# x1 through memory, and three more experts' weights in its room, in a one-core mixer and MoE layer

## The reference, cut to what matters

```
h  = rmsnorm(x, g_mix);  z = h @ w_in                 # 8 groups of 256 columns
mix = concat(conv A, pooling B, conv C, spatial gating D)
x1 = x + mix @ w_out                                  # the projection
h2 = rmsnorm(x1, g_ffn)
group = argmax(h2 @ rg_w);  two experts of its eight by h2 @ re_w
moe = sum over the two experts of gate * (silu(h2 @ w_gate[e]) * (h2 @ w_up[e])) @ w_down[e]
y  = rmsnorm(x1 + moe, g_final)
```

## Time and profile before

| | |
|---|---|
| median of 3 runs | 653.86 us (653.0 to 654.6) |
| profiled execution | 653.97 us, its span 652.1 us |
| busy: TensorE, VectorE, ScalarE, GpSimd | 557.4, 489.3, 278.6, 106.7 us |
| DMA | 116.33 MB, mean 178 GB/s |
| mean granted TensorE clock | 0.940 of full |

### The profile page before, as it was taken

One profiled execution on the slowest core, in us unless ns is written; L12 is line 12 of the kernel. 1 busy time (PEld: TensorE's weight loads), 2 busy tenths in 40 slices (PEclk: granted clock), 3 DMA queues, 4 the chain that ended last, 5 costly groups with the idle time before them and its releaser, 6 DMA issues.

```text
span 652.1 us, 10367 instructions
## 1 busy us (share of the span) xinstructions
PE 557.4 (85%) x3411; PEld 488.3 (75%) x3411; DVE 489.3 (75%) x758; ACT 278.6 (43%) x425; POOL 106.7 (16%) x150
## 2 busy tenths in 40 slices
PE   3899999999999998999999835999999999995000
PEld 2899999998898896888888525888888888883000
DVE  4947997999998668366655766888888888883597
ACT  5742112320313354312112125777777777773132
POOL 4300002000000000000000002233344444441000
PEclk9999999999999999999999956999999999999555
DMA  8660210111203103454211288799999999931884
GB/s 321 145 133 16 65 33 23 44 54 34 64 9 131 64 7 131 187 213 151 90 64 49 79 292 259 241 330 374 324 351 365 394 382 377 349 140 28 333 334 155
DMA packets 51445, 116.33 MB, mean 178 GB/s; under 512 B 8435, under 2 KB 26744, under 8 KB 50296
## 3 DMA queue, kind: packets, MB, share of 16 engines
q1 hardware_dynamic: 42899, 92.82, 41.1%
q0 software_dynamic: 6656, 17.84, 8.0%
q10 hardware_dynamic: 1828, 4.96, 2.1%
HBM read 99.75 MB, written 20.68 MB: 185 GB/s over the span
## 4 chain that ended last, share of the span: by engine, by line
PE 57%; DVE 19%; ACT 2%; DMA 2%; issue 2%; POOL 0%; POOLq 0%; DVEq 0%; ACTq 0%
PE ps L1942 14%; PE ps L2060 9%; PE ps L1765 8%; PE ps L2039 5%; PE ps L2020 5%; PE ps L2038 5%; PE ps L2040 5%; DVE at_x L1693 4%; PE ps L1983 2%; DVE at_mixP L1236 2%; DVE at_x L1701 2%; DVE at_hT L1196 1%; PE ps L1721 1%; DVE at_lnsq L1421 1%; DMA at_opair_p<-scratch_out 1%
## 5 line engine op out<-in xcount | busy, mean ns | idle before, releaser
L1765 PE MATMUL ps<-at_hT,at_ring 128*128 128x384 f32 x936 | 165.7, 333 | 1.1 <-ACT at_wk L641 1.1
L1765 PEld LDWEIGHTS ps<-at_hT,at_ring 128*128 128x128 f32 x936 | 155.8, 188 | 6.5 <-issue 5.0
L1942 PE MATMUL ps<-at_hT,at_mring 128*128 128x512 f32 (+1 forms) x432 | 102.6, 393 | 1.9 <-DVE at_mring L1389 1.2
L1942 PEld LDWEIGHTS ps<-at_hT,at_mring 128*128 128x128 f32 (+1 forms) x432 | 77.3, 182 | 21.1 <-DVE at_mring L1389 1.6
L2038 PE MATMUL ps<-at_whi,at_hTm 128*128 128x256 f32 x280 | 81.8, 292 | 0.0
L1236 DVE SCALAR_TENSOR_TENSOR at_mixP<-at_uc,sb_par,at_mixP 128x1024 f32<-128x1024 f32 x60 | 77.4, 1289 | 2.1
L2040 PE MATMUL ps<-at_whi,at_hTm_lo 128*128 128x256 f32 x280 | 78.8, 281 | 0.0
L1583 DVE TENSOR_TENSOR at_hTm_lo<-ps,at_hTm 128x1024 fp32r<-128x1024 f32 x35 | 42.9, 1225 | 21.6 <-ACT at_hTm L881 21.6
L1590 DVE TENSOR_TENSOR at_wlater_lo<-at_wlater,at_whi 128x1024 fp32r<-128x1024 f32 x40 | 49.0, 1226 | 9.6 <-ACT at_whi L889 7.9
L2020 PEld LDWEIGHTS ps<-sb_ident,at_xg 128*128 128x128 f32 x280 | 37.3, 190 | 24.6 <-issue 21.6
L2038 PEld LDWEIGHTS ps<-at_whi,at_hTm 128*128 128x128 f32 x280 | 53.5, 191 | 0.2 <-issue 0.2
(11 more groups left out here) (247 smaller groups left out, 859.4 us busy)
## 6 DMA issues: line engine op xcount, KB each, us to landing
at_wlater<-in_expert_w_gate SPq DMA_DIRECT2D x20, 512.0 KB
at_wlater<-in_expert_w_up SPq DMA_DIRECT2D x20, 512.0 KB
at_wlater<-in_expert_w_down SPq DMA_DIRECT2D x20, 512.0 KB
at_raw<-in_w_in SPq DMA_DIRECT2D x16, 512.0 KB, 3.9
at_opair_p<-scratch_out SPq DMA_DIRECT2D x8, 1024.0 KB, 12.4
at_wfirst<-in_expert_w_gate SPq DMA_DIRECT2D x15, 512.0 KB
at_wfirst<-in_expert_w_up SPq DMA_DIRECT2D x15, 512.0 KB
at_wfirst<-in_expert_w_down SPq DMA_DIRECT2D x15, 512.0 KB
```

Of the source, the lines that this page charges most:

```text
L1765: mm = pe.matmul(ps[:, bank + r, 0:t1 - t0], w[:, wpart, k * P:(k + 1) * P], hT[:, hpart, k, t0:t1], start=(m, wpart, hpart) == (0, 0, 0), ...
L1942: mm = pe.matmul(ps[0:n, b + r, :], mring[:, 1 - i % 2, mpart, k * P:k * P + n], wo[:, wpart, k, r * 512:(r + 1) * 512], start=(c, mpart, ...
```

## The change

x1 of each tile is written to a new tensor in memory (`xs`) right behind the tile's h. Once a tile's store has landed, its room, which is exactly one matrix wide, takes one matrix of experts 0 to 2 (`first_matrix`; tile t takes matrix t mod 3 of expert t div 3). The ring of eight slots starts with expert 3: expert b lies in slot (b-3) mod 8. Experts 3 to 5 are loaded at the first three tiles, 6 when the projection is done, 7 behind the last tile, 8 to 10 when the first gather has landed, and the rest as before when the expert eight earlier is done. When the last weights are issued and expert 2 is done, SyncE reads the nine tiles of x1 back to where they were, and VectorE waits for each of them in the last stage.

```
+            def store_rows(i):
                 sp.wait_ge(s["h2_ready"], i + 1)
                 sp.dma_start(hs[i * P:i * P + rows(i), :], wk[0:rows(i), i % 2, 0:D])...
+                sp.dma_start(xs[i * P:i * P + rows(i), :], x1[0:rows(i), i, :])\
+                    .then_inc(x1_stored[i % 2], 16)
+
+            def first_matrix(t):
+                sp.wait_ge(x1_stored[t % 2], 16 * (t // 2 + 1))
+                load_matrix(0, t // 3, t // 3, t % 3)
...
             for i in range(TILES):
                 if i == LAST:
                     sp.wait_ge(s["o_done"], TILES)
-                    expert_block(0, FIRST, FIRST, first=True)
-                store_h2(i)
+                    load_expert(0, 2 * FIRST, 2 * FIRST)
+                store_rows(i)
                 if i < FIRST:
-                    expert_block(0, i, i, first=True)
+                    load_expert(0, FIRST + i, FIRST + i)
+                if i >= 1:
+                    first_matrix(i - 1)
                 if i + 2 < TILES:
                     reload_x(i + 2)
...
-            for j in range(FIRST + 1, FIRST + 3):
-                expert_block(0, j, j, first=True)
+            load_expert(0, 2 * FIRST + 1, 2 * FIRST + 1)
+            first_matrix(LAST)
 
             sp.wait_ge(gath[0], 16)
-            for j in range(FIRST + 3, LAP):
-                expert_block(0, j, j, first=True)
-            with sp.Fori(1, NE // LAP) as i:
+            for j in range(2 * FIRST + 2, FIRST + LAP):
+                load_expert(0, j, j)
+            for j in range(FIRST, LAP):
+                expert_block(1, j, LAP + j)
+            with sp.Fori(2, NE // LAP) as i:
                 for j in range(LAP):
                     expert_block(i, j, i * LAP + j)
...
+            sp.wait_ge(s["d_done"], FIRST)
+            for n in range(2):
+                sp.wait_ge(x1_stored[n], 16 * ((TILES + 1 - n) // 2))
+            for i in range(TILES):
+                sp.dma_start(x1[0:rows(i), i, :], xs[i * P:i * P + rows(i), :]).then_inc(x_in[i], 16)
             sp.wait_ge(s["moe_done"], 1)
...
                     dve.wait_ge(pair_in[i], 16)
+                    dve.wait_ge(x_in[i], 48)
```

Which room and which semaphore belong to a block follows from new functions (`wexp(i, j)`, `weights_in(i, j)`), used by all engines:

```
+        def once(i, j):
+            return isinstance(i, int) and i * LAP + j < FIRST
+        def weights_in(i, j):
+            if once(i, j):
+                return once_in[j], 16, 0
+            return w_in_sem[(j - FIRST) % LAP], 16, i + (j - FIRST) // LAP
```

More of the change, by code:

```diff
@@ L145, in build_layer, with slot_of, wexp, wexp_lo @@
         o_xg = o_ring
[L146 to L155, removed]
+        wring = [at("wring_x", [P, FIRST, 3 * D], o_x1), at("wring_h", [P, LAP - FIRST, 3 * D], o_hT),
+                 at("wonce", [P, FIRST, 3 * D], o_mix)]
+        wring_lo = [at("wring_x_lo", [P, FIRST, 3 * D], o_x1, F32R),
+                    at("wring_h_lo", [P, LAP - FIRST, 3 * D], o_hT, F32R),
+                    at("wonce_lo", [P, FIRST, 3 * D], o_mix, F32R)]
+        def once(i, j):
+            return isinstance(i, int) and i * LAP + j < FIRST
+        def slot_of(parts, i, j):
+            if once(i, j):
+                return parts[2][:, j, :]
+            n = (j - FIRST) % LAP
+            return parts[0][:, n, :] if n < FIRST else parts[1][:, n - FIRST, :]
+        def wexp(i, j):
+            return slot_of(wring, i, j)
+        def wexp_lo(i, j):
+            return slot_of(wring_lo, i, j)
         whi = [at("whi0", [P, 2, KC // 2, FF], o_raw + D * 2, F32R),
@@ L161, in half @@
             return x[:, 0:2 * D].rearrange("p (g k f) -> p g k f", g=2, k=KC)[:, :, h * 4:h * 4 + 4, :]
-        def wexp_lo(j):
-            j %= LAP
-            return wfirst_lo[:, j, :] if j < FIRST else wlater_lo[:, j - FIRST, :]
         xg = at("xg", [P, XG, D], o_xg)
@@ L286, in build_layer @@
         hs = nc.dram_tensor("scratch_h", [NT, D], F32, kind="Internal").ap()
+        xs = nc.dram_tensor("scratch_x1", [NT, D], F32, kind="Internal").ap()
         orow = nc.dram_tensor("scratch_out", [2 * NT, D], F32, kind="Internal").ap()
@@ L308, in build_layer @@
         w_in_sem = [sem(f"expert_in{i}") for i in range(LAP)]
+        once_in = [sem(f"first_experts_in{i}") for i in range(FIRST)]
+        x1_stored = [sem(f"x1_stored{i}") for i in range(2)]
         gath = [sem(f"gathered{i}") for i in range(XG)]
@@ L413, in zf_wait, with weights_wait @@
             eng.wait_ge(s["zf_" + Z_USER[n]], nth(Z_USER, n))
-        def lap(i, j):
-            return i + j // LAP
+        def weights_in(i, j):
+            if once(i, j):
+                return once_in[j], 16, 0
+            return w_in_sem[(j - FIRST) % LAP], 16, i + (j - FIRST) // LAP
+        def weights_wait(eng, i, j):
+            arrived, each, turn = weights_in(i, j)
+            eng.wait_ge(arrived, 3 * each * turn + 3 * each)
         def result_out(eng, i):
@@ L513, in _, with load_matrix, load_expert, expert_block @@
                 load_piece(NPIECE + c)
[L515 to L526, removed]
+            def load_matrix(i, j, e, m):
+                w = ("expert_w_gate", "expert_w_up", "expert_w_down")[m]
+                src = a[w][0, bass.ds(e, 1), :, :].rearrange("o (q k) f -> q (o k f)", q=P)
+                sp.dma_start(wexp(i, j)[:, m * D:(m + 1) * D], src).then_inc(weights_in(i, j)[0], 16)
+            def load_expert(i, j, e):
+                for m in range(3):
+                    load_matrix(i, j, e, m)
+            def expert_block(i, j, e):
+                sp.wait_ge(s["d_done"], i * LAP + j - LAP + 1)
+                load_expert(i, j, e)
             def reload_x(i):
@@ L532, in reload_x @@
                 load_x(i, x1)
-            def store_h2(i):
+            def store_rows(i):
                 sp.wait_ge(s["h2_ready"], i + 1)
@@ L885, in expert_whi @@
                 b = i * LAP + j
-                act.wait_ge(w_in_sem[j % LAP], 48 * lap(i, j) + 48)
+                weights_wait(act, i, j)
                 if not (isinstance(b, int) and b < 1):
                     act.wait_ge(s["gu_done" if h else "gu_half"], b)
-                nc.scalar.activation(whi[h][:], half(wexp(j), h), ACT.Copy).then_inc(s[f"w_hi{h}"], 1)
+                nc.scalar.activation(whi[h][:], half(wexp(i, j), h), ACT.Copy).then_inc(s[f"w_hi{h}"], 1)
             def expert_silu(i, j):
@@ L1589, in expert_wlo @@
                 dve.wait_ge(s[f"w_hi{h}"], b + 1)
-                v.tensor_tensor(half(wexp_lo(j), h), half(wexp(j), h), whi[h][:].bitcast(F32),
+                v.tensor_tensor(half(wexp_lo(i, j), h), half(wexp(i, j), h), whi[h][:].bitcast(F32),
                                 ALU.subtract).then_inc(s[f"w_lo{h}"], 1)
@@ L2035, in expert_GU @@
                         pe.wait_ge(s[f"w_lo{h}"], b + 1)
-                    high, low = whi[h][:, :, k % 4, :], half(wexp_lo(j), h)[:, :, k % 4, :]
+                    high, low = whi[h][:, :, k % 4, :], half(wexp_lo(i, j), h)[:, :, k % 4, :]
                     x, x_low = hTm[:, j % 2, k, :], hTm_lo[j % 2][:, k, :]
@@ L2059, in expert_D @@
                     q = 2 * D + r * 512
-                    mm = pe.matmul(ps[:, 5 + r, :], actT[:, j % 2, :], wexp(j)[:, q:q + 512],
+                    mm = pe.matmul(ps[:, 5 + r, :], actT[:, j % 2, :], wexp(i, j)[:, q:q + 512],
                                    start=True, stop=True)
```

## The result

The changed kernel takes 656.65 us (median of 6 runs, 655.79 to 657.21) against 653.43 for the one before (6 runs, 652.91 to 654.6). The ratio is 1.0047, 95% interval 1.0037 to 1.0057: it is 3.1 us slower. The forecast of no change, the likeliest case, did not happen; the case beside it did, at the place that it named.

A forecast was written before the change was run, and what follows sets the result against it. TensorE was taken to set the pace, 5.53 us a step, with no wait for weights. Terms 0 + 0 + 0 + 0 + 0.6 gave +0.6 us: median 654.5 us, own range 653.2 to 655.1, 8 in 10 range 652.9 to 657.8.

The forecast's parts named there:

- The forecast of no change: Whole kernel: TensorE's pace of 5.53 us a step and its cover stand; 653.2 to 655.1 us, chance 0.50.
- the case beside it: Experts 31 to 34, 577 to 592 us: reads delay the last gathers and scatters, 1.3 to 3.9 us slower, chance 0.38.
- Steps 1 to 3: Three experts more ahead; x1 stores and piecewise loads in the projection; the turn from projection to experts: 0 us each.
- The cover of step 1: Expert stage: the DMA debt stays about 17 us short of starving TensorE, so 18 us more lead buys 0 us.
- Step 4: Reading x1 back from about 560 us: landed by about 587, before VectorE's addition at 610.69; cover 23 us, cost 0.
- Step 5: What the reads collide with, 565 to 587 us: last gather and scatters delayed, 0 to 3.9 us, taken as 0.6.
- The slack of the first copy: ScalarE's copy of expert 30's result, ending at 579.61, needed by TensorE at 581.53: 1.9 us slack, 0 to 0.9 lost.
- The second scatter: Issued at 579.09, has to be in 7.4 us later, before the down product at 587.09: 0 to 1.6 us lost.
- The bound of 9.0 us for a scatter under load: Full stretch: a scatter issued at 491.67 was done when its buffer was used at 500.69, so at most 9.0 us.
- The upper end of 3.9: Top of the loss at the last gathers and scatters: gather 0 to 2.9 us, GpSimd's gather issue at most 1.0 more.
- The rule of taking turns: A DMA engine alternates between queues packet by packet, so the last gather's data take about twice as long: sum 0 to 0.6.
- The memory latency at high load: 0.2 us on average, 2 at high load: each last gather or scatter 1.8 us later, sum nearer to 2.

The follow-up runs named there:

- experiment 1: The changed kernel without the nine reads of x1 (the last stage adds the first expert row twice instead): 653.62 us, ratio 0.9997.
- experiment 2: The changed kernel with the nine reads of x1 issued right behind the weights of expert 15: 661.58 us, ratio 1.0110.
- experiment 12: The kernel before, with each weight issued two down products (11.1 us) later: 659.87 us, ratio 1.0099.
- experiment 4: The kernel before, with the nine stores of x1 and the nine reads back added, no weight moved: 656.86 us, ratio 1.0041.
- experiment 3: The changed kernel with the reads of x1 waiting for the down product of expert 31: 654.61 us, ratio 1.0010.
- experiment 9: The changed kernel with ScalarE's copy of a result alone put behind the activation copy: 656.12 us, ratio 1.0045.

## Why the prediction failed where it did

*Steps 1 to 3: right in effect.* The lead is worth nothing (experiment 1), the stores are hidden (the 14.1 us a tile stand, and share 0.42 is the 0.4 that was worked out), and the first gather, at the turn, is 0.2 us longer (4.53 for 4.35), not shorter. Experts 8 to 10 go out from 395.03 on.

*The cover of step 1: mis-sized.* Before, weights are not 17 but about 5 us from being late (experiments 2 and 12). I took the drain behind the last issue, 16 us, for the whole stage. It was read at the stage's end; the first weights to be late were wanted at 515 us in experiment 2 and at 532 in experiment 12. Had the reads been put there, the prediction would have missed by 7 us. It made no difference to the sum, since the change leaves the ring as deep as it was.

*Step 4: right.* The last read of x1 lands at 593.7 us (issued at 572.4, 21.3 us to landing), 7 us later than the 587 of the forecast, but long before VectorE's first addition at 613.86; the last stage waits for the pairs, as before.

*Step 5: the place right, the size wrong.* The term was 0.6 us and measures 3.8 on TensorE (3.1 in the ratio). Three parts of it failed. (a) The slack of the first copy was given as 1.9 us, from its end (579.61) to TensorE's use. But the copy is not all that TensorE needs: behind it on ScalarE's queue stand 1.0 us of rows and 0.3 of activations, so the slack was 0.6; in experiment 1 the copy starts 0.6 later, at 579.62, and TensorE is just on time. (b) The second scatter was given a slack of 7.4 us by the same count and has 6.0 (from its issue at 579.09 to 587.09, less 2.0 for copy, rows and activations). It took 8.7 and was issued 0.2 later against TensorE's pace: 2.9 us. These are the 1.2 and 1.7 of the first two places together: "a stall at one place gives the next its time" held for them, and the second scatter alone would have cost as much. The 0.9 us that it costs through VectorE were in no term. (c) I took the low end "because the last gather and scatters are small". The last gather is: the trace before has seven packets of 4 KB for it. But the scatter of expert 29 is a full one, 128 packets of 4 KB, and small size is no safety either: the small gather landed 5.8 us after its issue in the kernel after and 2.6 without the reads (experiment 1).

The bound of 9.0 us for a scatter under load, read off a buffer's reuse in mid-stage, was good (7.9 and 8.7). With the right slack it would have given up to 9.0 - 6.0 = 3.0 us at the second scatter.

*The upper end of 3.9 held by luck.* It was 2.9 for the last gather and 1.0 for GpSimd's issue of a gather. The gather cost nothing in the kernel after, and the issue took 0.94 us in the full engines (at 578.15) as it did before (at 577.11), so that traffic was not what made another one 1.93. The scatters, which cost the 3.8, had 0.9 and 1.6 as their ends. The measured 3.1 lies in the range stated, by this sum and not by a right size of the terms.

*The rule of taking turns*, weighed in step 5 (the Trainium skill, "DMA: Bandwidth & Descriptors", section "Queues, rings and completion order"), gave 0 to 0.6 and missed. The scatter of expert 29 went from 4.5 us at most to 8.7, over 4 us more (from 3.6 in experiment 1, 5.1 more), where a doubled transfer would be some 1.4 more (0.52 MB at 380 GB/s). The memory latency at high load that the Trainium skill gives on the same page ("Latency and other measured facts"), by an estimate 1.8 us more, gave "nearer to 2" and is closer; both together are 3.2 us. Experiment 1 gives the landings without reads: 2.6 us for the last gather, seven packets of 4 KB, and 3.6 for the scatter of expert 29, 128 of them; in the kernel after they are 5.8 and 8.7. The gather is 3.2 us later with next to no data, so a doubled data time isn't the whole; the scatter's 1.9 beyond that is near the 1.4 of a doubling. What the 3.2 consist of, queueing, descriptors or memory, no run here tells.

*Why nothing was won.* The experts' weights were never late before, so no lead can be sold. The best version with the lead (experiment 1, which leaves x1 out) is level with the kernel before, and the cheapest place found for the reads costs 0.7 us (0.1 to 1.2). No version here beats it.

## What to carry to other kernels

Loading ahead pays only if somebody waits for the load: look at the reader's releasers first, and get the depth of the cover by making it smaller on the chip, not from how long the queue takes to drain. A transfer that nobody waits for still has a price where it fills engines that a late transfer needs; price that at the loaded latency, read from the busiest stretch, and ask of each transfer how late its issuer is. Slack is counted to the consumer through everything that stands behind the waiting instruction on its queue.

## What the runs showed of the hardware

On the indirect queue, a gather of seven rows landed 2.6 us after its issue and a scatter of 128 rows (0.52 MB) 3.6 us after, with no reads beside them (experiment 1); under the queue of reads they took 5.8 and 8.7 (after) and 5.8 and 8.3 (experiment 4). The scatter of expert 28 took 6.2 to 6.6 without reads (before, experiments 1 and 3) and 7.6 to 8.4 with them (after, experiments 4 and 9). And a debt of the DMA engines lasts: 4.46 MB put in at 452 us made the first weight late at 515 us, with the engines at a share of 1.03 in all of the time between.
